# DeltaNet projections: VectorE alone forms the remainders of the weight units

## The reference, cut to what matters

```python
def gated_deltanet(h, w_in, conv_w, A_log, dt_bias, norm_w, w_out):
    proj = h @ w_in
    qkv, z, b, a = jnp.split(proj, ...)
    qkv = lax.conv_general_dilated(qkv, conv_w ...)     # 4 taps, per channel
    qkv = jax.nn.silu(qkv)
    q, k, v = jnp.split(qkv, ...)
    q = l2_normalize(q) * GDN_DK ** -0.5
    k = l2_normalize(k)
    beta, g = sigmoid(b), -exp(A_log) * softplus(a + dt_bias)
    o = chunk_gated_delta_rule(q, k, v, g, beta)        # (I + A) is solved, A strictly lower
    o = rms(o) * norm_w * jax.nn.silu(z)
    return o.reshape(B, S, GDN_V_W) @ w_out
```

## Time and profile before

| | |
|---|---|
| time, median of 3 runs | 1102.07 us (1100.94 to 1103.49) |
| profiled execution, its own time | 1101.09 us |
| its span, first to last instruction | 1099.3 us |
| PE busy | 1066.4 us (97%) |
| PE's weight load busy | 899.8 us (82%) |
| DVE busy | 610.6 us (56%) |
| ACT busy | 530.0 us (48%) |
| POOL busy | 106.5 us (10%) |
| mean granted clock of PE | 0.989 of 2.4 GHz |
| DeltaNet in the span | about 672 to 905 us |

### The profile page before, as it was taken

The page is one execution under the profiler, slowest core; times in us unless marked ns, Lnnn a source line. Parts: engine busy times, 40 slices in busy tenths (PEclk is TensorE's granted clock), DMA queues, the critical chain, the costliest instruction groups (busy, mean ns, idle before and its releaser), DMA issues.

```text
span 1099.3 us, 14631 instructions
## 1 busy us (share of the span) xinstructions
PE 1066.4 (97%) x5500; PEld 899.8 (82%) x5500; DVE 610.6 (56%) x829; ACT 530.0 (48%) x778; POOL 106.5 (10%) x117
## 2 busy tenths in 40 slices
PE   9999999987999999999999998999998999999997
PEld 7888888855888888888888887979997988888885
DVE  5555454668564555446555545683595466455542
ACT  8453443545563535336534435673466346353531
POOL 0000000342000000000000005550333100000000
PEclk9999999999999999999999999998998999999999
DMA  9746465331446555546465553320430065565520
GB/s 330 237 163 206 175 224 195 127 116 39 153 157 210 168 201 215 187 123 224 159 200 182 223 195 111 128 77 1 148 146 15 25 206 172 168 214 193 217 87 38
DMA packets 123694, 174.68 MB, mean 159 GB/s; under 512 B 7280, under 2 KB 97664, under 8 KB 123648
## 3 DMA queue, kind: packets, MB, share of 16 engines
q1 hardware_dynamic: 121120, 171.99, 45.9%
q10 hardware_dynamic: 2528, 2.06, 0.6%
HBM read 172.98 MB, written 1.05 MB: 158 GB/s over the span
## 4 chain that ended last, share of the span: by engine, by line
PE 88%; DVE 7%; ACT 3%; POOL 1%; issue 1%; ACTq 0%; DVEq 0%; POOLq 0%
PE bank L1357 25%; PE bank L1359 25%; PE bank L1358 25%; PE bank L1660 4%; PE bank L1431 2%; PE bank L1631 1%; PE bank L1654 1%; DVE w_lo L959 1%; PE bank L1388 1%; PE bank L1745 1%; DVE prob L1153 1%; DVE X L1276 1%; ACT y_sb L654 1%; ACT w_hi L643 1%; PE bank L1570 0%
## 5 line engine op out<-in xcount | busy, mean ns | idle before, releaser
L959 DVE TENSOR_TENSOR w_lo<-w_raw,w_hi 128x2048 fp32r<-128x2048 f32 x151 | 360.6, 2393 | 152.8 <-ACT w_hi L643 152.5
L643 ACT ACTIVATE w_hi<-w_raw 128x2048 fp32r<-128x2048 f32 x159 | 304.0, 1919 | 116.0 <-PE bank L1359 115.5
L1357 PE MATMUL bank<-w_hi,xT_hi 128*128 128x512 f32 x784 | 312.5, 399 | 1.1 <-DVE w_lo L1085 0.8
L1359 PE MATMUL bank<-w_hi,xT_lo 128*128 128x512 f32 x784 | 306.0, 390 | 0.0
L1358 PE MATMUL bank<-w_lo,xT_hi 128*128 128x512 f32 x784 | 305.4, 390 | 0.0
L1357 PEld LDWEIGHTS bank<-w_hi,xT_hi 128*128 128x128 f32 x784 | 147.3, 188 | 32.7 <-issue 2.7
L1359 PEld LDWEIGHTS bank<-w_hi,xT_lo 128*128 128x128 f32 x784 | 147.1, 188 | 31.5
L1358 PEld LDWEIGHTS bank<-w_lo,xT_hi 128*128 128x128 f32 x784 | 147.4, 188 | 29.6 <-issue 0.7
L685 ACT ACTIVATE silu_g<-bank,rstd 128x256 f32<-128x256 f32 x88 | 36.9, 471 | 247.8 <-PE bank L1359 247.8
L1357 PE MATMUL bank<-w_hi,hT_hi 128*128 128x512 f32 x352 | 138.1, 392 | 0.0
L1359 PE MATMUL bank<-w_hi,hT_lo 128*128 128x512 f32 x352 | 137.1, 390 | 0.0
(11 more groups left out here) (271 smaller groups left out, 1109.0 us busy)
## 6 DMA issues: line engine op xcount, KB each, us to landing
w_raw<-in_ffn_w_gate_up SPq DMA_DIRECT2D x170, 512.0 KB, 4.8
w_raw<-in_ffn_w_down SPq DMA_DIRECT2D x88, 512.0 KB, 4.1
w_raw<-in_gdn_w_in SPq DMA_DIRECT2D x32, 512.0 KB, 4.5
w_raw<-in_attn_w_in SPq DMA_DIRECT2D x12, 512.0 KB, 4.3
w_raw<-in_attn_w_out SPq DMA_DIRECT2D x8, 512.0 KB, 4.0
w_raw<-in_gdn_w_out SPq DMA_DIRECT2D x8, 512.0 KB, 5.2
w_raw<-in_ffn_w_gate_up SPq DMA_DIRECT2D x12, 256.0 KB, 5.0
x_sb<-in_x SPq DMA_DIRECT2D x4, 256.0 KB, 4.8
```

What stands on the lines that cost most here:

```text
L643: act.activation(w_hi[u0 % RING][:], w_raw[u0 % RING][:], ACT.Copy).then_inc(hi_ready, 1)
L959: dve.tensor_tensor(w_lo[u0 % RING][:], w_raw[u0 % RING][:], w_hi[u0 % RING][:].bitcast(F32), ALU.subtract).then_inc(split_ready, 1)
L1357: pe.matmul(out_ap, a[0], b[0], start=start, stop=False, **kw)
L1359: return pe.matmul(out_ap, a[1], b[0], start=False, stop=stop, **kw)
```

## The change

The eight remainders that POOL formed are formed by DVE. There is one count for all units, `split_ready`, and the semaphore `pool_split`, the table and the function `splits` are gone. On DVE the new remainders stand right behind the old ones: the unit with the next number after the taps of q, after the taps of k, after the last level of the inverse, and after the finished output. On POOL nothing takes the place of the removed ones.

```diff
-POOL_UNITS = [U_GDN + 5 + 2 * n for n in range(4 * NG)]
-
-
-def splits(u):
-
-    by_pool = sum(v <= u for v in POOL_UNITS)
-    return by_pool if u in POOL_UNITS else u + 1 - by_pool
...
-            if u0 in POOL_UNITS:
-                eng.wait_ge(pool_split, splits(u0))
-            else:
-                eng.wait_ge(split_ready, splits(u0) + 4 * i)
+            eng.wait_ge(split_ready, u0 + 1 + 4 * i)
...
                 if g:
                     pool.wait_ge(R_psum, TT * g)
                     decay_rows(g)
-                split_lo(U_GDN + 8 * g + 5)
                 if g == 0:
                     pool.wait_ge(gate_dve, GATE_G)
                     decay_rows(g)
-                split_lo(U_GDN + 8 * g + 7)
                 for t in range(TT):
...
-                split_lo(U_GDN + 8 * g + 9)
                 pool.wait_ge(g_loaded, 16 * G_LOADS)
...
-                split_lo(U_GDN + 8 * g + 11)
...
                 if part < 2:
                     split_lo(U_GDN + 2 * n + 4)
+                    split_lo(U_GDN + 2 * n + 5)
...
                 split_lo(U_GDN + 8 * g + 8)
+                split_lo(U_GDN + 8 * g + 9)
                 dve.wait_ge(O_psum, TT * g + 1)
...
-                split_lo(U_GDN + 8 * g + 10)
+                for n in range(10, 12):
+                    split_lo(U_GDN + 8 * g + n)
```

More of the change, by code:

```diff
@@ L280, in build @@
         split_ready = sem("split_ready")
-        pool_split = sem("pool_split")
         unit_done = sem("unit_done")
@@ L596, in _ @@
             z.then_inc(g_masks, 1)
[L598 to L602, removed]
             def decay_rows(g):
```

## The result

The changed kernel takes 1090.15 us (median of 4 runs, 1089.92 to 1094.07) against 1102.59 us before (4 runs, 1100.94 to 1103.49). The ratio is 0.9897, with an interval of 0.9883 to 0.9911: 11.3 us faster, between 9.8 and 12.9. The two medians lie 12.4 us apart; the ratio is worked out from all the executions, the one at 1094.07 us too. The forecast was 1089.7 us. The profiled execution took 1090.30 us, its span is 1088.5 us.

What follows compares the result with a forecast made beforehand. PE bounds the kernel, busy 1066.4 of 1099.3 us; DVE and POOL stop each other, delaying `X`. Gains 0.7 + 1.7 + 2.3 + 3.6 + 4.0 + 0.1 = 12.4 us give 1089.7 us, range 1088.5 to 1098.8.

Steps and rivals of the forecast that it cites:

- Remainders: Eight remainders move to DVE at 2.28 us each, 18.2 us; two in 4.48 us replace one of 6.21 behind taps.
- The gates: Group 0, behind the remainder: DVE 1.7 us earlier covers PE's 0.6 us wait; gain taken as 0.7 us.
- `X`, group 0: `X` ends at 741.0 against 742.72, each `gU` hold taken as 0.2 us; gain 1.7 us, between 2.3 and 0.6.
- The rival of the whole-length hold: `gU` holds DVE for its whole length; `X` of group 0 ends at 742.1, clock falls there: 1094.9 us, chance 0.08.
- `X`, group 1: Same as in group 0 but no decay rows behind; ends at 838.7 against 840.99, gain 2.3 us.
- The clock: Shorter PE gaps at `X` keep the granted clock up, so dense work behind takes half; gain 3.6 + 4.0 us.
- The comparison row: PE at 675.15 to 680.45, busy 2.06 of 5.3 us with a 1.9 us gap, clock at 1.00.
- the 0.4 us a group: Estimated cost behind `X`: at full clock PE meets DVE's two L1283, which the slow clock hid.
- Behind the inverse: DVE copies the output row until 780.2, ACT busy until 780.89: cost 0, 0.7 us spare; decay rows leaving gain 0.1.
- Behind the output: `g_oT_lo` slides by 2.2 us to 892.5 in group 1, needed at 893.1: cost 0, with 1.2 us to spare.
- The rival of a clock fall that stays: One clock fall stays, most likely in group 0: gain 8.3 us, 1093.8 us, chance 0.28.
- The slower rival: Output row becomes late behind the inverse, once the copy of `Lm` ends over 0.7 us later: 1111 us, chance 0.05.

Runs made afterwards that it cites:

- the filled kernel: Kernel before, with PE's two waits for `X` in each group filled by 14 and 16 identity transposes that nothing reads: 1094.95 us, ratio 0.9941.
- the doubled remainder: Changed kernel with the second unit's remainder behind the inverse formed twice in each group, 2.28 us more on DVE: 1091.22 us, ratio 0.9908.
- the execution of 1093.28 us: Slowest of six executions when the changed kernel was measured again, nothing altered; that set's median 1089.37 us, ratio 0.9897 against the kernel before.
- the first two experiments: Kernel before with only some remainders moved to DVE: units 5, 7, 13, 15 (1101.70 us, ratio 0.9992); only units 9, 17 (1090.57 us, ratio 0.9898).
- the later remainders: Changed kernel, but POOL forms units 9, 11, 17 and 19, with 9 and 17 only once `X` is done: 1089.48 us, ratio 0.9884.

## Why the prediction was right

The time, 1090.15 us, lies 0.45 us from the forecast. The gain forecast was 12.4 us; the medians lie 12.4 us apart, and the ratio gives 11.3 (9.8 to 12.9). The steps hold in size one by one; the reason given for the fifth does not.

1. *Remainders.* Two in 4.48 us where one took 6.14 to 6.21, as costed, in all four places behind the taps.
2. *The gates.* 0.7 us forecast, 0.9 measured. PE's wait is gone.
3. *`X`, group 0.* 1.7 us forecast, 2.2 measured. The mis-sized term is what a `gU` costs DVE: I took 0.2 us for each of three instructions, from the small L1319, and it is 0.05 us once and nothing twice. The floor was nearly right. It was POOL that waited: one `gU` beside `X` is 1.32 us long, where its median is 0.61. PE's waits for `X` sum to 2.9 us where I had 3.7. The rival of the whole-length hold falls.
4. *`X`, group 1.* 2.3 forecast, 2.3 measured.
5. *The clock.* 7.6 us forecast, 7.1 measured in the profile, and 6.5 (4.7 to 8.4) by the filled kernel alone. But the reason that I gave, that no new gap is longer than one of 1.9 us which had left the clock up, is not sound. In the changed kernel's two profiles the same gap at the entry once let the clock fall and once not, and so did single gaps of 1.8 to 2.0 us between the groups of one execution. Over the eleven profiles in which the gap at the entry is not filled, the clock fell behind it in four. The comparison row had been a lucky one. The conclusion held: in all five profiles in which the gaps at `X` are 0.8 and 0.7 us the clock stays at 1.00 from 738 to 855. That this is because they are so much shorter is likely; no run has there, as its longest gap, one between 0.84 and 1.8 us. And the 0.4 us a group that I set against the gain for L1283 (L1260 now) was put at the wrong place: PE waits 0.2 us a group for ACT's `XT` and not for `Lm`.
6. *Behind the inverse.* No cost, as forecast. I named ACT as the cover, 0.7 us; DVE's own wait for PE, 1.07 us, is the one that the doubled remainder used up, and 2.3 us more cost 1.1 a group in the profiles.
7. *Behind the output.* `g_oT_lo` had room: PE's list shows no wait for it. The loads cost nothing that shows.

The rival of a clock fall that stays did not come about in either group in the two profiles of the changed kernel. For the execution of 1093.28 us, one of ten, it is not excluded: that rival's time was 1093.8. The slower rival needed a copy more than 0.7 us late; even 2.3 us late cost only 1.1 us a group. That the total agrees so closely is partly luck: 1.8 us lie against the change in the first profile, most of them the bad luck of the clock's fall at the entry, and a median of four moves by a microsecond with it. The kernel before measured 0.5 us slower than the median that the forecast started from.

## What to carry to other kernels

Before work is spread over DVE and POOL, look at what the other one does at the same moment. Here a long POOL instruction on SBUF operands held DVE until its end when DVE came to read two SBUF operands (4.87 us in place of 0.69), the short `gU` cost it 0.05 us beside `X`, and instructions of DVE that take one operand from PSUM lost nothing (0.42 us). So two badly placed instructions out of eight were the whole measurable loss. Two waits of PE of 2.0 and 1.4 us cost about three and a half more in each group through the clock; a single one cost nothing, or by estimate up to three (6.4 us of dense work at 0.51 instead of 1.00). Read the granted clock in the stretch behind each gap before you price it. Filling the gap with transposes that nothing reads tests this in one edit, and here it was worth about half of what the real change brought, or somewhat more.

## What the runs showed of the hardware that was not expected

- *DVE's instructions, following each other closely, kept POOL's `gU` out.* Beside `X` eight `gU` took 6.05 us in place of 4.66, while DVE's four instructions lost 0.05 us. The longer norm weights, before, had got in between the same instructions one by one. Why these got in and `gU` did not, no run shows.
- *The clock at the same gap differs between executions and between groups.* At the entry, 1.00 in one and 0.50 for over 3 us in the other, with the same waits of 1.4 and 1.9 us. The four profiles with this fall are the changed kernel's first, those of the first two experiments and that of the later remainders; the page of a single execution can't price such a gap.
